# Three of five token tiles take their expert sums from whole tables instead of fetched rows

## What is computed

```python
def peer_ffn(h, p):                      # U, V: 16384 experts x 1024
    q = (x @ p['peer_wq'])               # 8 heads x 2 halves of 128
    s1, s2 = scores of each half against 128 keys
    v1, i1 = top_k(s1, 16); v2, i2 = top_k(s2, 16)
    best, pos = top_k(v1[:, None] + v2[None, :], 16)   # 16 pairs per head
    idx = i1 * 128 + i2 at pos           # 8 x 16 = 128 experts per token
    g = softmax(best)
    act = gelu(einsum('nhkd,nd->nhk', U[idx], x))
    return einsum('nhk,nhkd->nd', g * act, V[idx])
x = x + gate2 * peer_ffn(h2, p)
```

## Time and profile before

| | us |
|---|---|
| median of 3 runs | 5405.83 (5401.6 to 5411.79) |
| span of the profiled execution | 4934.2 |
| TensorE busy | 3129.1 |
| VectorE busy | 3893.0 |
| GpSimd busy | 2774.2 |
| ScalarE busy | 766.9 |

### The profile page before, as it was taken

The page is one execution under the profiler, slowest core; times in us unless marked ns, Lnnn a source line. Parts: engine busy times, 40 slices in busy tenths (PEclk is TensorE's granted clock), DMA queues, the critical chain, the costliest instruction groups (busy, mean ns, idle before and its releaser), DMA issues. The chain is left out here.

```text
span 4934.2 us, 39343 instructions
## 1 busy us (share of the span) xinstructions
PE 3129.1 (63%) x11894; PEld 1694.5 (34%) x11894; DVE 3893.0 (79%) x7442; ACT 766.9 (16%) x1900; POOL 2774.2 (56%) x2867
## 2 busy tenths in 40 slices
PE   8989879987055073277978996999713606407137
PEld 3368846542011021023425884754201202102012
DVE  6947665997997997978754766599899799798875
ACT  2112252211010010012111225221100101001001
POOL 0013240767777777766661334066777777777775
PEclk9999969999588597698998996999957958759669
DMA  8700011999999999999993001289999999999998
GB/s 308 233 17 2 4 50 67 367 410 407 410 408 399 409 406 401 409 406 384 417 382 126 2 1 36 78 315 409 409 410 409 400 410 405 407 406 399 410 407 357
DMA packets 434890, 1491.66 MB, mean 302 GB/s; under 512 B 47213, under 2 KB 55525, under 8 KB 433911
## 3 DMA queue, kind: packets, MB, share of 16 engines
q0 software_dynamic: 368640, 1342.34, 68.6%
q1 hardware_dynamic: 66040, 146.81, 8.4%
HBM read 1480.92 MB, written 5.44 MB: 301 GB/s over the span
## 5 line engine op out<-in xcount | busy, mean ns | idle before, releaser
L2072 PE MATMUL ps<-z,o 128*128 128x512 f32 x2356 | 1168.7, 621 | 1541.0 <-DMA z<-in_peer_v,experts 1485.5
L2115 DVE CUSTOM_DVE_ANT_0 z<-z,ps 128x1024 f32<-128x1024 f32 x1176 | 1409.8, 1218 | 69.3 <-DMA z<-in_peer_u,experts 34.4
L1775 POOL DMA_INDIRECT z<-in_peer_u,experts x1176 | 1112.2, 946 | 481.7 <-issue 225.3
L1775 POOL DMA_INDIRECT z<-in_peer_v,experts x1178 | 1131.9, 961 | 425.7 <-issue 281.9
L2072 PEld LDWEIGHTS ps<-z,o 128*128 128x128 f32 x2356 | 410.6, 193 | 2291.5 <-issue 1720.2
L2148 DVE SCALAR_TENSOR_TENSOR ps<-z,state,ps 128x1024 f32<-128x1024 f32 x579 | 745.6, 1288 | 331.1 <-DMA z<-in_peer_v,experts 330.9
L1902 ACT ACTIVATE o<-const,state 128x128 f32<-128x128 f32 x640 | 244.7, 398 | 1139.9 <-PE ps L2072 1087.4
L848 POOL TENSOR_TENSOR kn<-kn,neg_half 128x4 f32<-128x4 f32 x20 | 20.1, 1007 | 341.8 <-DVE kn L891 313.2
L858 POOL TENSOR_TENSOR w<-w,const 128x512 f32<-128x512 f32 x60 | 86.5, 1446 | 209.9 <-DVE w L880 117.8
L463 DVE SCALAR_TENSOR_TENSOR o<-gate,cond,o 128x1024 f32<-128x1024 f32 x160 | 192.5, 1278 | 9.9 <-DMA gate<-in_w_mod 9.7
L858 POOL TENSOR_TENSOR hT<-hT,const 128x512 f32<-128x512 f32 x60 | 85.5, 1430 | 199.5 <-DVE hT L880 103.7
(11 more groups left out here) (443 smaller groups left out, 5265.7 us busy)
## 6 DMA issues: line engine op xcount, KB each, us to landing
gate<-in_w_mod SPq DMA_DIRECT2D x80, 512.0 KB, 4.5
w<-in_w_in SPq DMA_DIRECT2D x12, 2048.0 KB, 10.9
z<-in_peer_v,experts POOLq DMA_INDIRECT x1178, 13.3
z<-in_peer_u,experts POOLq DMA_INDIRECT x1176, 13.4
z<-in_peer_wq SPq DMA_DIRECT2D x4, 2048.0 KB, 15.5
rows<-in_peer_wq SPq DMA_DIRECT2D x4, 2048.0 KB, 16.6
w<-in_peer_wq SPq DMA_DIRECT2D x4, 2048.0 KB, 17.5
rows<-in_w_in SPq DMA_DIRECT2D x3, 2048.0 KB, 18.9
```

The lines of the kernel that those rows point to most:

```text
L1775: eng.indirect_dma_start(slot, None, at_layer_rows(table), bass.IndirectOffsetOnAxis(ap=m.experts[:, t % 2, k:k + 1], axis=0)).then_inc(lo ...
L2072: mm = eng.matmul(m.ps[:, 4 + n, :], m.diag[:, (done + q) % DIAGS, :], row_j[:, n * 512:(n + 1) * 512], start=(q == 0), stop=(q == SLOTS / ...
L2115: eng.tensor_tensor_reduce(row_j, row_j, h_rows, 1.0, 0.0, ALU.mult, ALU.add, m.acts[:, k:k + 1]).then_inc(used_v, 1)
```

## The change

Tiles 0 and 1 go on fetching rows (`FETCHED`), tiles 2 to 4 don't (`DENSE`, 384 tokens). The tiles are ranked in the order 0, 2, 3, 4, 1.

For a dense tile the kernel builds a matrix of gates, 128 first keys x 128 second keys for each token, which holds the token's softmax shares at its experts. `keep_turned` and `turn_keys` turn a tile's key numbers and shares so that the 128 slots lie on partitions. `onehots` (VectorE) and `first_onehot` (ScalarE, for every second build) write one-hot rows of 4 tokens; `build_gates` multiplies them, four products of 128 columns for 4 tokens; `keep_build` evicts. The gates go to DRAM in chunks of 32 tokens, 2 MB each, 12 a layer.

Then come 128 blocks, one for each first key: `dense_products(b)` multiplies 128 rows of U (from a transposed copy, `peer_ut`, a new input made on the host) with the 384 tokens, ScalarE and VectorE apply gelu and gates to the 128 x 384 results, and `dense_sums(b)` adds their products with 128 rows of V to six banks of PSUM. Blocks stand behind rows 34 to 252 of the 256 rows of tile 1, by `block_behind`. SyncE streams U (4 buffers), V (3) and gates (groups of 8 blocks).

For tile 0, TensorE now adds all 128 V rows, for tile 1 VectorE does. The ring has 8 slots. `project_ahead` is gone: `stage_norm_project` does all five tiles, with context and latent columns evicted by ScalarE and VectorE.

```diff
-RING, DIAGS = 13, 8
+RING, DIAGS = 8, 8
-PROJECTED_AHEAD = TILES - 1
-    tiles = list(range(PROJECTED_AHEAD, TILES))
-        blocks = [(n, t, min(512, D_IN - n * 512)) for n in range(NB) for t in tiles]
+        blocks = [(n, t, min(512, D_IN - n * 512)) for n in range(NB) for t in range(TILES)]
...
+FETCHED, DENSE = (0, 1), tuple(range(2, TILES))
+RANK_ORDER = (0, 2, 3, 4, 1)
+CHUNK, SUB = 32, 4
+CHUNKS, SUBS = NT // CHUNK, P // SUB
+GROUP = 8
+TABLE_U, TABLE_V = 4, 3
+def block_behind(b):
+    return 34 + (b * (2 * SLOTS - 36)) // NKEY
...
+                def store_gates(c):
+                    d, last = c * CHUNK // P, (c * CHUNK % P + CHUNK) // SUB - 1
+                    eng.wait_ge(*unit_kept("unit", build_unit(d, last)))
+                    eng.dma_start(m.dense_gates[c], m.gate_chunk[c % 2]).then_inc(gates_stored[c % 2], 16)
+                def load_u(b):
+                    if b >= TABLE_U:
+                        eng.wait_ge(*unit_made("unit", block_unit(b - TABLE_U)))
+                    eng.dma_start(m.table_u[b % TABLE_U], m.inp["peer_ut"][l, b]).then_inc(u_loaded[b % TABLE_U], 16)
...
+                def first_onehot(d, b):
+                    for i in range(SUB):
+                        at = d * P + b * SUB + i
+                        ins = eng.activation(m.first_onehot[0][:, i, :], const(m, "iota"), ACT.Abs, bias=m.slot_rows[:, 0, at:at + 1], scale=-1.0)
...
+                        ins = eng.activation(to, to, ACT.Relu, bias=m.slot_rows[:, 2, at:at + 1], scale=m.minus_share[:, at:at + 1])
+                def keep_block(b):
+                    if b > 0:
+                        dense_tanh(b - 1)
...
+                    eng.activation(m.dense_acts[b % 2], acts, ACT.Copy).then_inc(acts_kept, 1)
+                    eng.activation(m.dense_inner[b % 2], acts.rearrange("p (d t) -> p d t", d=ND), ACT.Square, scale=0.044715 ** 0.5).then_inc(
+                        unit_kept.sem, unit_kept.one("unit", u))
...
+                def build_gates(d, b):
+                    for i in range(SUB):
+                        mm = eng.matmul(to[:, i * P:(i + 1) * P], m.second_onehot[n % 2][:, i, :], m.first_onehot[n % 2][:, i, :], start=True, stop=True)
+                def dense_products(b):
+                    for c in range(KC):
+                        mm = eng.matmul(to[:, 0:NT], m.table_u[b % TABLE_U][:, c, :], m.hT[:, c, D0:TOK], start=(c == 0), stop=(c == KC - 1))
+                def dense_sums(b):
+                    eng.wait_ge(acts_ready, b + 1)
+                    eng.wait_ge(v_loaded[b % TABLE_V], 16 * (b // TABLE_V + 1))
+                    for d in range(ND):
+                        for n in range(2):
+                            mm = eng.matmul(m.ps[:, 2 * d + n, :], m.dense_acts[b % 2][:, d * P:(d + 1) * P], m.table_v[b % TABLE_V][:, n * 512:(n + 1) * 512],
+                                            start=(b == 0), stop=(b == NKEY - 1))
...
+                for b in range(NKEY):
+                    dense_products(b)
+                    if b > 0:
+                        dense_sums(b - 1)
...
+                def onehots(d, b):
+                    if n % 2 == 1:
+                        for i in range(SUB):
+                            ins = eng.tensor_scalar(m.first_onehot[1][:, i, :], const(m, "iota"), m.slot_rows[:, 0, at + i:at + i + 1],
+                                                    m.slot_rows[:, 2, at + i:at + i + 1], ALU.is_equal, ALU.mult)
+                    eng.tensor_tensor(m.second_onehot[n % 2], bc(const(m, "iota"), 1, SUB), bc(m.slot_rows[:, 1, at:at + SUB], 2, NKEY),
+                                      ALU.is_equal).then_inc(second_ready, 1)
+                def dense_block(b):
+                    if b > 0:
+                        gate_acts(b - 1)
...
+                for k in range(SLOTS):
+                    dot(1, k)
+                    if k < SUBS:
+                        onehots(2, k)
...
+                    for b in BLOCK_BEHIND[k]:
+                        dense_block(b)
```

More of the change, by code:

```diff
@@ L85, in constants @@
     put("blocks", (s // HD == t // HD))
-    put("sixteen", np.tile(np.arange(16), (P, 1)))
+    put("iota", np.tile(np.arange(128), (P, 1)))
     pos = np.arange(DEC)
@@ L1651, in stage_experts @@
[L1651 to L1661, removed]
-        in_scaled, in_turned = Marks(sem("next_tile_scaled"), "tile"), Marks(sem("next_tile_turned"), "tile")
@@ new lines, in _ @@
+                load_scores(1)
+                load_scores(2)
+                for d in range(ND):
+                    for c in range(CHUNKS // ND * d, CHUNKS // ND * (d + 1)):
+                        store_gates(c)
+                    if d < ND - 1:
+                        load_scores(d + 3)
+                for stored in gates_stored:
+                    eng.wait_ge(stored, 16 * CHUNKS // 2)
+                eng.wait_ge(*unit_made("unit", build_unit(ND - 1, SUBS - 1)))
+                load_gates(0)
@@ L1911, in _ @@
+                dense_tanh(NKEY - 1)
             @block.tensor
@@ L2160, in _, with rank, spread_steps @@
+                def rank(pos, first, last):
+                    for i in range(first, last):
+                        rank_step(eng, m, o, sems, pos, i)
                 SPREAD = 2 * TOPK
                 GATE_BEHIND = {1: 3, 6: 4, 11: 5, 17: 6, 20: 7, 22: 8, 24: 9}
-                for i in range(HEAD_PAIR_STEPS):
-                    rank_step(eng, m, o, sems, 0, i)
+                def spread_steps(k):
+                    i = HEAD_PAIR_STEPS * (1 + k // SPREAD) + k % SPREAD
+                    return k >= SPREAD and k % SPREAD < HEAD_PAIR_STEPS and i < RANK_STEPS - SHARE_STEPS, i
@@ new lines, in _ @@
+                cube(1, 1)
+                for k in range(SLOTS):
+                    if k == LATE_HALF:
+                        weigh(1, 1)
+                    add_row(k)
+                    for b in BLOCK_BEHIND[SLOTS + k]:
+                        dense_block(b)
+                gate_acts(NKEY - 1)
+                eng.wait_ge(used_v, rows_used(NROWS - 1)[0])
+                residual(1, m.row_sum)
+                eng.wait_ge(v_used, NKEY)
+                for d, t in enumerate(DENSE):
+                    residual(t, sum_in_banks(2 * d))
```

592 lines of the change are left out of this document (345 added, 247 removed).

## The result

The changed kernel takes **5755.9 us** (median of 4 runs, 5751.3 to 5757.5) against 5403.7 for the kernel before beside it (4 runs, 5400.3 to 5411.8): a ratio of 1.0651, 95% interval 1.0636 to 1.0666, 352 us slower. Forecast were 6230 us, range 6100 to 6450. The direction was right, the time was outside the range. The profiled execution took 5756.7 us, 1.8 above its span.

The account below looks back on a forecast made before the run. The kernel before was taken as bound by its row transfers, the changed blocks by TensorE. Losses of 318.5, 336.7, 155 and 12 us on a span of 4934.2 gave 5756, plus 471.6 carried over 6230; range 6100 to 6450.

Parts of the forecast that it names:

- the last of the sum: Outside the profiled span: the 471.6 us between span and median of the kernel before carried over, 5756 to 6230.
- The rival on this part: Time outside the span grows, with the span (+79 us) or the input bytes (+171): 6310 to 6400; chance 0.12.
- a block: Streamed blocks of tiles 2 to 4: TensorE sets the pace at 10.44 us each, 1336 us for 128.
- first block: After tile 0's values, gate builds, tile 1's start and the gates' store and load: blocks begin at T+497.
- stage between the layers: Between layers 0 and 1, now projecting five tiles: 211 us instead of 55.4, 155 more.
- ring: Row slots in the dot phases: 8 for 13 lose five rows of prefetch, 6 us a layer, 12 in all.
- The product's price: TensorE's cost of a product: 0.867 us with 512 columns, 0.655 estimated with 384.
- The first rival: In the blocks, TensorE keeps up with the streams: transfers set 5.3 us a block, 4904 us total; chance 0.03.
- The chain over ScalarE and VectorE: In the blocks: forecast 6.8 us within 10.4; as rival it sets 12.4 a block, about 6740 us; chance 0.07.
- The builds: Gate builds before the blocks: ranking and one-hots 99 us to T+356, ScalarE's work taken as hidden, bounds 0 to +90 a layer.
- the third rival: Gate builds wait on ScalarE, one after another: 2 to 3 us more a pair, +130 to +190, about 6390; chance 0.15.
- No projection ahead: Projection moved from layer 0's experts to between the layers: 155 us more there, removal in layer 0 worth nothing.

Follow-up runs that it names:

- sitting of 4937.6: A stretch of runs on one chip in which the kernel before took 4937.6 us; the changed kernel, unchanged, took 5728.6 beside it, ratio 1.160.
- 5754.9 trace: The changed kernel's profiled execution with a span of 5754.9 us, from the first sitting: median 5755.9 us beside 5403.7 for the kernel before.
- 5726.8 trace: The changed kernel, unchanged, run again where the kernel before took 4937.6 us: 5728.6 us, ratio 1.160.
- sittings of 4940: Four of the eight stretches of runs on one chip, in which the unchanged kernel before took some 4940 us; in the other four it took some 5410.
- 5416.2 trace: The kernel before, unchanged, run again for a profile and a time of the same execution: 5414.8 us, beside 5417.4.
- the one with 8 slots at 5338.2: The kernel before with 8 row slots instead of 13, in a long sitting: 5343.8 us beside 5403.0, ratio 0.9903.
- two-dense kernel: Two tiles on the streamed tables instead of the changed kernel's three: 4899.9 us beside 4940.2 for the kernel before, and 4928.9 beside 5418.5.

## Why the prediction failed, by its own steps

**The step that failed is the last of the sum**: "The median of the runs, 5405.8, is 471.6 us above the profiled span; ... so I carry 471.6 over". The difference was not time around the span, for which 1.8 us were measured with both kernels. It was the kernel before itself, slower in the sitting where it was timed than in its trace. A trace of such a sitting has 482 us more, and they lie in what the change removes or shrinks: fetched rows at 1.43 us instead of 1.30 (218 in the seven plain tiles), ScalarE's lateness in tile 4 beside the projection ahead (117 with that tile's rows), and the first tile's value rows (118); the other 29 lie ahead of T. The changed kernel fetches 512 rows a layer for 1280, most of them beside a full TensorE, has no projection ahead, and had 29 us of it. The two summands excluded each other: whoever carries 471.6 us over must not also remove what they were spent on. The rival on this part let it only grow, and its lower bound was "no change in it or a little less"; that it could vanish had no price.

The sum on the span held: 5756 forecast, 5754.9 measured. Partly by luck, since its base was a trace of the other kind. In the trace of the changed kernel from the sitting of 4937.6 the span is 5726.8, so against 4934.2 it grows by 793 us where 822 were forecast. Its terms (T is the end of the first tile's dots: 1078.2 and 3916.0 in the 5754.9 trace, 1074.0 and 3895.6 in the other):

| term | forecast | measured (5754.9 trace) | (5726.8 trace) |
|---|---|---|---|
| a block | 10.44 | 10.30 | 10.31 |
| value phase with early builds | T+256 | T+264.7 | T+254.9 |
| first block | T+497 | T+501.7 | T+494.0 |
| end of the layer's experts | T+1840 | T+1832.9, T+1834.7 | T+1825.7, T+1827.1 |
| stage between the layers | 211 | 204.7 | 203.9 |
| ring (T, and T of layer 1 from its stage, later) | 12 | 12 and 16, like the kernel before there | 8 and 8 |

- **The product's price** carried the forecast and held: 0.857 for 0.867, and 0.645 for the estimated 0.655. The first rival (TensorE keeps up with the streams) is refuted: over 1100 us without idle time the products come 1% closer together, not 40%. Of the two figures of the Trainium skill (TensorE: Matmul & The Clock Gate, Back-to-back issue gap) that the prediction weighed, the isolated gap of about 216 ns is near what was measured, 0.857 us over the four passes that the prediction counts, 214 ns. Nothing here shows 131.
- **The chain over ScalarE and VectorE** stayed below: in 1700 to 2800 TensorE waits for nobody.
- **The builds** cost what was forecast, with other shares: from the value phase to the first block 237 us for 241. Two groups of the changed kernel in 1190 to 1580, TensorE's with the wait for ScalarE that the third rival named:

```profile
L2165 PE MATMUL ps<-w,z 128*128 128x128 f32 x762 | 140.2, 352 | 100.1 <-ACT w L1936 57.7 <-DVE z L2317 39.7 <-ACT z L1945 2.4
L1936 ACT ACTIVATE w<-w,slot_rows,rows 128x128 f32<-128x128 f32 x188 | 77.4, 482 | 1.6
```

  ScalarE's operations take 0.48 and 0.39 us where 2.9 / 8 was counted, and its eviction of a build, written across a chunk, 1.06 for 0.6. The sum still came out, so the extra 130 us never came; which of the waits (58 us for ScalarE, 40 for VectorE) stood in for which term wasn't taken apart.
- **No projection ahead**: 148 to 149 us more in the stage for 155. What comes back in layer 0, 23 us in sittings of 4940, was put at nothing.
- **The ring**: in the 5726.8 trace T comes 8 and 8 us later than in the trace, 16 for 12. In the kernel before, where all ten tiles live by it, the same 8 slots cost 25 to 30.

Measured against the kernel before of its own kind of sitting (the 5416.2 trace, where the experts' parts take 1787.5 and 1690.4 us from T on, and the stage 55), the 338.7 us between the spans are: layer 0 +45.4, the stage +149.4, layer 1 +144.3, which is all of it within a microsecond. So in such a sitting most of the loss is the stage that now projects all tiles, and layer 1's blocks. Layer 0's blocks cost little, because they replace the tile in which VectorE waited 99 us for ScalarE.

## What to carry to other kernels

Before anything is added to a profiled span, ask whether the profiled execution is one of the timed ones; a gap of 9% is a different execution until shown otherwise, and then it belongs to what was slower in it, not outside. An exchange of fetched rows for a stream that all tokens share pays only as far as TensorE has room: with three tiles a block took 10.3 us, all of them TensorE's, with the DMA engines busy 0.62; with two it took 8.0, of which TensorE worked 7.3, with a DMA share of 1.00. Only the second is a gain, under 1% or 9% by the sitting. A measured ratio between a transfer-bound and a TensorE-bound kernel (1.064 or 1.160 here) holds for the sitting in which it was taken.

## What the runs showed of the hardware

The same kernel, bound by row transfers, ran at 5403 to 5418 us in four sittings and at 4938 to 4940 in four (medians), each time within 0.5% in a sitting. In a window of 800 us (1450 to 2250) the 4 KB packets have a median of 159 to 160 ns in both kinds, but 2.7% of them (1,946 of 71,387) took over 300 ns in the 5416.2 trace and 2.5% in the one with 8 slots at 5338.2, against 0.4% (286 of 77,937) in that of 4934.2. Their mean is 173 ns for 164, about half of the difference between 365 and 405 GB/s. Long packets alone don't mark a long sitting: the changed kernel has 7.4% in both kinds. What makes them long, and why the two-dense kernel (1.5%, and 1.3% in the other kind) loses only 29 us by it, is open. That the long sittings spare traffic which mixes SyncE's table pieces with GpSimd's rows fits 388 GB/s beside 368, and was not tried by itself.

The DMA share doesn't stand for bytes alone: fetched rows had 405 GB/s at a share of 1.02, the changed kernel's blocks 208 GB/s at 0.62, which would be 335 at 1.00 (estimate). The prediction's "DMA share at half" came from bytes, and was low for that reason.
